# Two gate products of the merge stage ahead of the short convolution's output products, and the later gate products one pair earlier

## The reference

```
def conv_mixers(h, w_in, cf_b_pw1, sc_conv_w, sc_w_out, cf_conv_w, cf_conv_b, cf_ln_g, cf_ln_b,
                cf_w_pw2, cf_b_pw2, w_mix_out):
    proj = jnp.einsum('bsd,dc->bsc', h, w_in)
...
    sc_b, sc_c, sc_x, cf_a, cf_g, gate_sc, gate_cf = jnp.split(proj, cuts, axis=-1)
    y_sc = sc_b * causal_depthwise_conv(sc_c * sc_x, sc_conv_w)
    y_sc = jnp.einsum('bsc,cd->bsd', y_sc, sc_w_out)
    cf = (cf_a + cf_b_pw1[:CF_WIDTH]) * jax.nn.sigmoid(cf_g + cf_b_pw1[CF_WIDTH:])
    cf = causal_depthwise_conv(cf, cf_conv_w) + cf_conv_b
    cf = jax.nn.silu(layer_norm(cf, cf_ln_g, cf_ln_b))
    y_cf = jnp.einsum('bsc,cd->bsd', cf, cf_w_pw2) + cf_b_pw2
    merged = jax.nn.sigmoid(gate_sc) * y_sc + jax.nn.sigmoid(gate_cf) * y_cf
    return jnp.einsum('bsd,de->bse', merged, w_mix_out)
```

## Time and profile before

| | us |
|---|---|
| Median of 3 runs (lowest, highest) | 3608.92 (3606.71, 3617.18) |
| The profiled execution | 3611.44 |
| Its span, first to last instruction | 3609.6 |
| PE busy | 3311.6 (92%) |
| DVE busy | 2553.1 (71%) |
| ACT busy | 1537.4 (43%) |
| POOL busy | 781.3 (22%) |

### The profile page before, as it was taken

How to read it: one execution, slowest core, us unless ns; L and a number is a source line. 1 busy time by engine, 2 the same in 40 slices (tenths; PEclk the granted TensorE clock), 3 DMA queues, 4 the chain that set the end, 5 groups by cost and what they waited for, 6 DMA issues and landing times.

```text
span 3609.6 us, 50438 instructions
## 1 busy us (share of the span) xinstructions
PE 3311.6 (92%) x18674; PEld 2622.5 (73%) x18674; DVE 2553.1 (71%) x4528; ACT 1537.4 (43%) x3085; POOL 781.3 (22%) x577
## 2 busy tenths in 40 slices
PE   7998989978997776999899999888999999999998
PEld 6887779844552222788677776667899988898898
DVE  6997252866777876787767687777867576768665
ACT  3222344254443333444444454544545444444443
POOL 1000445043446664222122232122200000000000
PEclk9999999999999999999899999989999999999999
DMA  3222234489999998799788898878955744353455
GB/s 122 95 95 78 88 105 142 134 349 418 411 409 421 413 413 362 305 379 394 301 316 324 295 395 346 301 283 336 358 178 188 244 142 137 128 182 116 136 186 157
DMA packets 183454, 918.82 MB, mean 255 GB/s; under 512 B 21456, under 2 KB 26832, under 8 KB 117280
## 3 DMA queue, kind: packets, MB, share of 16 engines
q0 software_dynamic: 73728, 536.90, 37.3%
q1 hardware_dynamic: 99248, 358.66, 29.2%
q10 hardware_dynamic: 10240, 20.12, 1.7%
HBM read 907.80 MB, written 7.80 MB: 254 GB/s over the span
## 4 chain that ended last, share of the span: by engine, by line
PE 72%; DMA 9%; DVE 8%; issue 5%; ACT 4%; POOL 3%; ACTq 0%; DVEq 0%; POOLq 0%
PE psum L706 51%; PE psum L1051 11%; DMA buffer_float<-in_peer_uv,buffer_uint 7%; DVE buffer_bfloat L2510 2%; POOL buffer_float L3187 2%; PE psum L714 2%; DMA raw_slabs<-in_slabs 1%; ACT slabs_rounded L1416 1%; PE psum L1254 1%; DVE buffer_float32r L2124 1%; PE psum L1239 1%; DVE buffer_float L2178 1%; PE psum L1336 1%; PE psum L1300 1%; DVE buffer_float L2664 1%
## 5 line engine op out<-in xcount | busy, mean ns | idle before, releaser
L706 PE MATMUL psum<-buffer_float32r,slabs_rounded 128*128 128x256 f32 (+3 forms) x9504 | 1983.6, 308 | 58.4 <-DVE buffer_float32r L2124 34.2
L706 PEld LDWEIGHTS psum<-buffer_float32r,slabs_rounded 128*128 128x128 f32 x9504 | 1534.3, 191 | 212.4 <-issue 128.9
L706 PE MATMUL psum<-buffer_float32r,slabs_remainder 128*128 128x256 f32 (+3 forms) x4752 | 1422.9, 299 | 0.0
L2218 DVE TENSOR_TENSOR slabs_remainder<-raw_slabs,slabs_rounded 128x1024 fp32r<-128x1024 f32 x597 | 728.4, 1223 | 479.1 <-ACT slabs_rounded L1416 460.7
L1416 ACT ACTIVATE slabs_rounded<-raw_slabs 128x1024 fp32r<-128x1024 f32 x658 | 692.7, 1057 | 746.9 <-PE psum L706 636.2
L1051 PE MATMUL psum<-buffer_float,buffer_float 128*128 128x512 f32 x1712 | 830.1, 614 | 139.9 <-ACT buffer_float L1703 124.2
L706 PEld LDWEIGHTS psum<-buffer_float32r,slabs_remainder 128*128 128x128 f32 x4752 | 904.7, 190 | 29.2
L3187 POOL DMA_INDIRECT buffer_float<-in_peer_uv,buffer_uint x512 | 632.5, 1235 | 1346.7 <-PE psum L1051 800.7
L2510 DVE CUSTOM_DVE_ANT_0 buffer_bfloat<-buffer_float,buffer_float 128x1024 bf16<-128x1024 f32 x512 | 625.7, 1222 | 180.0 <-DMA buffer_float<-in_peer_uv,buffer_uint 173.7
L1051 PEld LDWEIGHTS psum<-buffer_float,buffer_float 128*128 128x128 f32 x1712 | 305.0, 194 | 524.3 <-issue 515.1
L1692 ACT ACTIVATE buffer_float<-buffer_float 128x1 f32<-128x1 f32 x512 | 100.6, 196 | 382.7 <-DVE buffer_float L2510 381.0
(11 more groups left out here) (213 smaller groups left out, 2022.1 us busy)
## 6 DMA issues: line engine op xcount, KB each, us to landing
raw_slabs<-in_slabs SPq DMA_DIRECT2D x682, 512.0 KB
buffer_float<-in_peer_uv,buffer_uint POOLq DMA_INDIRECT x512
buffer_float<-kept ACTq DMA_DIRECT2D x1, 5248.0 KB, 17.6
xT<-in_xT ACTq DMA_DIRECT2D x4, 512.0 KB, 6.0
buffer_float<-in_consts ACTq DMA_DIRECT2D x8, 256.0 KB
kept<-buffer_float ACTq DMA_DIRECT2D x4, 512.0 KB
kept<-buffer_float ACTq DMA_DIRECT2D x4, 272.0 KB
kept<-buffer_float ACTq DMA_DIRECT2D x8, 136.0 KB, 1.7
```

What stands on the lines that cost most here:

```text
L706: m = pe.matmul(out, a, b, start=start and j == 0, stop=stop and j == 2)
L2218: dve.tensor_tensor(slab_l[:, r, :], raw[:, r, :], slab_h[:, j, :].bitcast(F32), ALU.subtract)\
```

## The change

Products keep their number, but stand in another order, and the table `SOURCE`, which says which slab of the weights is sent as the n-th, follows it. Slabs 48 and 49 are now the first two gate products, 50 to 57 the eight short convolution products (with `column_sums` still behind the fifth of them and `mean_squares` behind the eighth), 58 and 59 the second pair of gates, 60 and 61 the first `cfs` pair, 62 and 63 gates, 64 and 65 `cfs`, 66 and 67 gates, 68 and 69 `cfs`, 70 and 71 `cfs`. On ACT the first two sigmoids stand in front of the norm, each with one slab rounded behind it; the norm rounds four slabs instead of two behind its squares. In the rounds the sigmoid of the next pair waits until DVE has used the gate that lies in the same buffer `xs`, that is, until the `cfs` product of this round has been consumed. DVE's fourfold hardware loop is written out.

```
-SOURCE = [*range(FIRST), *AGAIN, *range(FIRST, FIRST + BLOCK2), *range(FIRST, FIRST + BLOCK2)]
+GATED = 7 * KT
+GATES = [(GATED + 4 * i, GATED + 4 * i + 1) for i in range(KT // 2)]
+CFS = [(GATED + 4 * i + 2, GATED + 4 * i + 3) for i in range(KT // 2)]
+SOURCE = [*range(6 * KT), *GATES[0], *range(6 * KT, GATED), *GATES[1], *CFS[0], *GATES[2], *CFS[1], *GATES[3], *CFS[2],
+          *CFS[3], *range(GATED + 2 * KT, FIRST), *AGAIN,
...
@@ PE
+            for _ in range(2):
+                product(op)
             await_split()
...
-                for c in range(2):
+                for c in range(2 if i < 3 else 0):
                     product(op)
@@ ACT
-            split_ahead(3)
+
+            def gate(c, bn):
+
+                b = full(bn)
+                act.activation(xs[:, c, :], psum[:, b, :], ACT.Sigmoid).then_inc(bank_free[b], 1)
+
+            split_ahead()
+            for c in range(2):
+                gate(c, gm.take())
+                split_ahead()
...
-            norm(cfc, dst=None, last=2)
+            norm(cfc, dst=None, last=4)
...
-            for _ in range(4):
-                cf_gates = [gm.take() for _ in range(2)]
-                for c, gcf in enumerate(cf_gates):
+            for i in range(4):
+                cf_gates = [gm.take() for _ in range(2)] if i < 3 else []
+                for c in range(2):
                     ycf = gm.take()
-                    b = full(gcf)
-                    act.wait_ge(bank_free[ycf[0]], ycf[1] + 1)
-                    act.activation(xs[:, c, :], psum[:, b, :], ACT.Sigmoid).then_inc(bank_free[b], 1)
-                    split_ahead(2)
+                    if cf_gates:
+                        act.wait_ge(bank_free[ycf[0]], ycf[1] + 2)
+                        gate(c, cf_gates[c])
+                    split_ahead(2 if i < 3 else 1)
@@ DVE
+                if c == KT - 1:
+                    cf_gates = [gm.take() for _ in range(2)]
...
-            with repeat(dve, 4, [(gm, 4)]) as i:
-                cf_gates = [gm.take() for _ in range(2)]
+            for i in range(4):
+                next_gates = [gm.take() for _ in range(2)] if i < 3 else []
```

More of the change, by code:

```diff
@@ L180 @@
 SLABS = BLOCK1 + 2 * BLOCK2
-SOURCE = [*range(FIRST), *AGAIN, *range(FIRST, FIRST + BLOCK2), *range(FIRST, FIRST + BLOCK2)]
+GATED = 7 * KT
[3 more added lines that the diff above has]
+          *CFS[3], *range(GATED + 2 * KT, FIRST), *AGAIN,
+          *range(FIRST, FIRST + BLOCK2), *range(FIRST, FIRST + BLOCK2)]
 assert len(SOURCE) == SLABS
@@ L2306, in _ @@
                     dve.wait_ge(merged_done, i * 2 + (c + 1))
-                    dve.scalar_tensor_tensor(out=acc_o, in0=psum[:, b, :], scalar=vec_at("pw2_b", i, 2, c),
+                    dve.scalar_tensor_tensor(out=acc_o, in0=psum[:, b, :], scalar=vec("pw2_b", 2 * i + c),
                                              in1=xs[:, c, :], op0=ALU.add, op1=ALU.mult).then_inc(bank_free[b], 1)
                     dve.wait_ge(bank_free[b], ycf[1] + 2)
-                    m = row(merged, i * 2 + c, 0, S)
+                    m = merged[:, 2 * i + c, :]
                     dve.tensor_tensor(m, m, acc_o, ALU.add).then_inc(merged_done, 1)
+                cf_gates = next_gates
             for k in range(KT):
```

## The result

The changed kernel takes 3628.68 us (median of 7 runs, 3623.98 to 3634.46), the kernel before 3608.69 us (median of its 7 runs beside them). The ratio is 1.0050, with a 95% interval of 1.0039 to 1.0061, which is 18 us of 3608.69; the two medians alone stand 20.0 us apart. Forecast were 3632.8 us, in a range from 3626 to 3641.

The account below looks back on a forecast made before the run. PE, busy 92% of the span, was taken as the bound. A neutral reordering (+1.1 us) plus three stalls (3 x 7.6 = 22.8) gave +23.9 us on the median 3608.92: 3632.8 us, range 3626 to 3641.

Parts of the forecast that it names:

- Gate products in front: Start of the stage: PE's 6.46 us wait and its 2.5 us of slow clock go; `column_sums` at 335.2, 1.0 later.
- Slab 55: Behind `column_sums`: slab 55 starts at 350.2, with PE idle some 14 us ahead of it instead of 2.7.
- Mean squares: Three products behind slab 55's start instead of one: mean squares at 369.5, 13.1 us later than before.
- the slow clock behind the long wait: Behind PE's 14 us wait ahead of slab 55: 2.5 us lost, between 1.5 and 3.2.
- First cfs product: 15.8 us behind the mean squares, as before: starts at 385.3, 13.1 us later.
- Two products fewer behind it: Behind the first `cfs` product: 12 products instead of 14, 11.2 us less; with the 0.79 wait gone, 1.1 us later overall.
- Slabs 61, 65 and 69: Rounded behind a waiting sigmoid: PE idles 5.3 us at each, 7.6 with slow clock and overlap, 22.8 us in all.
- Slabs 63, 67 and 71: Ready 5.5 us behind the product's end, needed at 5.6: just in time, a few tenths each if POOL is slower.
- The rest: DVE's loop written out, dropped last gates, slab transfers and the wait of `w_mix_out`: no time.
- the faster one: ACT's order doesn't hold PE back, slab 55 is rounded before the squares: 16 us faster, 3593; chance 3%.
- the one with no change: The 14 us stall comes, but ACT regains a slab's lead behind slab 60: 1.1 us remain, 3610; chance 4%.
- The slower one: Slabs 63, 67 and 71 miss too, POOL and DVE meet, POOL taking over 2.5 us: +33, 3642; chance 8%.

Follow-up runs that it names:

- early: The changed kernel with slabs 55 to 58 rounded ahead of the wait for the centred tiles instead of behind the squares; ratio 1.0012 to the kernel before.
- lead: The changed kernel with five instead of four slabs rounded behind the squares, so slabs 61, 65 and 69 are rounded earlier; ratio 0.9994 to the kernel before.
- one_left: The changed kernel with one slab more rounded in the first round only, behind the second sigmoid; ratio 1.0014 to the kernel before.
- buffers: The changed kernel, roundings untouched, with the gates in two buffers by turns (`xs` and `sg`); ratio 0.9995 to the kernel before.
- both: The changed kernel with slabs 55 to 58 rounded ahead of the centred tiles' wait, 59 behind the squares, one slab of lead in the rounds; 3593.47 us, ratio 0.9951.
- tuned: The kernel with earlier sums, with slabs 55 and 56's remainders taken by DVE and 57 to 59 rounded behind the squares; 3588.82 us, ratio 0.9929 to the kernel before.

## Why the prediction was right, and where its sizes were off

The sign, the places and the causes came out as written. By its steps, read at the starts of PE:

1. *Gate products in front.* `column_sums` at 335.05 (forecast 335.2). DVE was idle from 330.3 on, waiting for `column_sums`, so PE sets this time.
2. *Slab 55.* 349.95 (350.2), with 13.88 us of idle time (14). The kernel with early rounding shows that ACT's order is the cause.
3. *Mean squares.* 368.53, 12.2 later than before where 13.1 was forecast. The term that was off in this execution is the slow clock behind the long wait. I took 2.5 us; the row below (window, length, busy by engine with counts, PEclk, DMA share, GB/s) shows three steps in 3.87 us instead of 2.1, so 1.8 us.

```profile
349.95:353.82 3.87, 3.87 (x9) 3.05 (x10) 1.10 (x2) 2.34 (x2) 3.87 (x2) 0.52 0.47 135
```

Three other kernels have the same wait of 13.9 us, and read in the same way they lose more: lead 2.1 us (four steps in 4.91 from 349.94), one_left 2.7 (five in 6.20 from 349.78), buffers 2.8 (five in 6.34 from 348.82). The 2.5 lies in the middle of the four.

4. *First cfs product.* 384.36, 15.8 us behind the mean squares, as forecast.
5. *Two products fewer behind it.* The kernel with the lead restored ends its stage at the very time of the kernel before (456.66), where 1.1 us more was forecast: neutral.
6. *Slabs 61, 65 and 69.* Idle 5.15, 4.84 and 4.84 us, forecast 5.3. At the latter two DVE began at once behind the product (421.59, PE idle from 421.56), not 0.4 us later. Slabs 63, 67 and 71 were in time. Behind slab 60 the chain of waits shows three entries of DVE's own sequencer between PE's end (391.75) and DVE's start (392.09), behind slab 64 none. With the slow clock the three cost 21.5 us together, forecast 22.8.
7. *The rest.* Nothing showed.

The sum at the end of the stage was 21.5 us, forecast 23.9; the medians differ by 20.0. The last 1.5 us between those two are inside the scatter of the runs.

One part of the agreement is luck. The prediction priced the slow clock of a stall between neighbours by the length of the wait. The runs show no such order (last section); the three stalls lost 2.2, 2.7 and 1.5 us, and only their mean is the 2.1 forecast.

Of the rivals, the faster one became real as soon as its condition was made true (kernel both), and the one with no change when the three stalls were taken away (lead, buffers). The slower one's condition, POOL taking 2.5 us or more in the stalls, didn't hold: it took 2.36. I added nothing for POOL beside DVE, and in the changed kernel that was right, for the two don't meet in the stalls: behind slab 64 DVE's addition is over at 423.07 and POOL starts at 423.99. Ahead of slab 55 they do meet (a remainder of 2.85 us at 347.06 beside DVE's sums of squares), but they did so before too, with 2.83, and the 15.0 us taken from there has it in it. But I had that cost in hand, in the addition of 2.37 us, and left it out of what I expected of the kernels that round slabs earlier. There it was worth about 2.2 us for each remainder and made the kernel with earlier sums miss.

## What to carry to other kernels

When products are moved past each other on one engine, move the work that prepares them too, and count its lead: for each product, how many slabs have been prepared at the moment the preparing engine stops to wait. Here the change filled a 6.5 us wait of PE and paid with 13.9 and 3 x 5 us elsewhere, because the preparer was stopped by waits it shares with other work; the same order with the slabs prepared earlier in both places (kernel both) is faster than the kernel before by 0.5%, and with the sums moved forward and the remainders kept out of DVE's way (tuned) by 0.7%. Before an engine's spare time is used for early preparation, see what runs beside it: POOL was idle there, but DVE paid.

## What was not expected of the hardware

POOL's remainder of a 128x1024 slab holds back DVE instructions on SBUF by nearly its whole length: 2.2 us for each, while DVE alone needs 1.14 us from start to start for the same remainder (2.35 us for two). Where the two meet, moving that work to the idle engine costs the busy one twice what it would have paid to do it itself.

The time lost to the slow clock does not grow with the wait. Behind 13.9 us idle PE lost 1.8, 2.1, 2.7 and 2.8 us in four kernels; behind two waits of the same 4.84 us it lost 2.7 and 1.5. These are the stretches behind the latter two (window, length, busy by engine with counts, PEclk, DMA share, GB/s), five steps in 6.20 us and three in 3.56, at 0.7 us a step with the full clock:

```profile
426.39:432.59 6.20, 6.20 (x15) 4.86 (x16) 0.00 (x0) 0.00 (x0) 2.27 (x1) 0.54 0.28 85
456.44:460.00 3.56, 3.56 (x10) 2.85 (x10) 0.00 (x0) 0.00 (x0) 2.27 (x1) 0.58 0.47 132
```

What sets which of the two it is stays open; no run here varied it. In the kernel early the same two waits lost 2.7 and 1.4. The price of a wait of PE in this stage was its length plus 1.4 to 2.8 us, whether it was short or long.
